# Level products of a blocked triangular inverse: from 64x64 weight tiles to 32x32 quarters with compact masks

## The reference, cut to what matters

```python
def step(s, inp):
    r_t, w_t, k_t, v_t, kk_t, a_t = inp
    sa = jnp.einsum('bhvk,bhk->bhv', s, -kk_t)
    s = s * w_t[:, :, None, :] + sa[..., None] * (kk_t * a_t)[:, :, None, :] + v_t[..., None] * k_t[:, :, None, :]
    return s, jnp.einsum('bhvk,bhk->bhv', s, r_t)
```

## Time and profile before

| quantity | value |
|---|---|
| median of 3 runs | 1657.73 us (1657.66 to 1657.81) |
| the profiled execution | 1657.09 us, span 1655.3 us |
| mean granted clock of TensorE | 0.948 |
| PE matmuls | 1465.5 us busy, 89% of the span, 17678 instructions |
| PE loads | 930.4 us, 56% |
| DVE | 605.6 us, 37%, 1520 instructions |
| ACT | 528.1 us, 32% |
| POOL | 264.7 us, 16% |
| level products of levels 1 to 4 (L2485), 881 to 1240 us | 3072 matmuls, 114.8 us busy |
| their mask on DVE (L2346) | 64 instructions, 0.52 to 0.56 us |

### The profile page before, as it was taken

The page is one execution under the profiler, slowest core; times in us unless marked ns, Lnnn a source line. Parts: engine busy times, 40 slices in busy tenths (PEclk is TensorE's granted clock), DMA queues, the critical chain, the costliest instruction groups (busy, mean ns, idle before and its releaser), DMA issues. The chain is left out here.

```text
span 1655.3 us, 41184 instructions
## 1 busy us (share of the span) xinstructions
PE 1465.5 (89%) x17678; PEld 930.4 (56%) x17678; DVE 605.6 (37%) x1520; ACT 528.1 (32%) x1202; POOL 264.7 (16%) x260
## 2 busy tenths in 40 slices
PE   3998878878999999959998888888879779999997
PEld 1554557446555555535556777777755555555554
DVE  2003673243111111551214666666751511111116
ACT  3013553232121121220134666666541311111122
POOL 0000031002000000010034455556500100000010
PEclk9999899888999999979999999999988889999999
DMA  9324556737799999803210000000004469999992
GB/s 390 128 102 164 221 210 244 300 115 315 278 369 379 374 377 373 332 26 102 103 50 3 6 6 6 6 6 6 6 4 170 154 267 364 374 370 380 375 387 90
DMA packets 54037, 328.34 MB, mean 198 GB/s; under 512 B 6646, under 2 KB 10038, under 8 KB 18712
## 3 DMA queue, kind: packets, MB, share of 16 engines
q1 hardware_dynamic: 43632, 290.07, 45.9%
q0 software_dynamic: 5184, 18.88, 2.9%
q10 hardware_dynamic: 5096, 17.58, 2.7%
HBM read 304.35 MB, written 22.16 MB: 197 GB/s over the span
## 5 line engine op out<-in xcount | busy, mean ns | idle before, releaser
L1398 PE MATMUL ps<-ring,arena 128*64 128x256 f32 x2048 | 244.3, 387 | 6.0 <-ACT arena L1513 4.9
L1398 PEld LDWEIGHTS ps<-ring,arena 128*64 128x64 f32 x2048 | 142.4, 138 | 97.2 <-issue 36.6
L298 PE MATMUL ps<-HT,ring 128*128 128x384 f32 x544 | 181.3, 497 | 14.2 <-PEq L367 8.2
L298 PEld LDWEIGHTS ps<-HT,ring 128*128 128x128 f32 x544 | 105.8, 195 | 89.5 <-issue 20.3
L1408 PE MATMUL ps<-ring,arena 128*32 128x128 f32 x4096 | 133.9, 278 | 0.0
L1602 DVE TENSOR_TENSOR arena<-arena,ps 64x256 f32<-64x256 f32 (+1 forms) x128 | 40.6, 357 | 254.0 <-ACT arena L1519 254.0
L1434 PE MATMUL ps<-ring,arena 128*64 128x512 f32 x512 | 129.9, 605 | 0.0
L1518 ACT ACTIVATE arena<-ps 64x256 f32<-64x256 f32 x64 | 24.1, 377 | 311.3 <-PE ps L1398 311.3
L1408 PEld LDWEIGHTS ps<-ring,arena 128*32 128x32 f32 x4096 | 107.8, 111 | 27.0 <-issue 25.4
L298 PE MATMUL ps<-arena,ring 128*128 128x384 f32 x256 | 85.4, 498 | 18.8 <-DVEq L2053 18.8
L1526 ACT ACTIVATE arena<-ps 32x256 f32<-32x256 f32 x128 | 47.8, 374 | 160.3 <-PE ps L1434 159.2
(11 more groups left out here) (358 smaller groups left out, 2244.2 us busy)
## 6 DMA issues: line engine op xcount, KB each, us to landing
ring<-wstream SPq DMA_DIRECT2D x272, 1024.0 KB, 7.5
moe_rows<-arena ACTq DMA_DIRECT2D x28, 384.0 KB, 7.1
arena<-moe_tokens POOLq DMA_DIRECT2D x12, 512.0 KB, 14.7
moe_rows<-arena ACTq DMA_DIRECT2D x4, 512.0 KB
consts<-cst ACTq DMA_DIRECT2D x1, 1655.0 KB, 17.1
XT<-xT ACTq DMA_DIRECT2D x1, 1536.0 KB, 11.1
yT<-HT SPq DMA_DIRECT2D x3, 384.0 KB, 3.2
arena<-wa SPq DMA_DIRECT2D x1, 1024.0 KB, 4.9
```

What stands on the lines that cost most here:

```text
L298: mm = pe.matmul(bank(m % 8), w[:, k, m % 2 * P:m % 2 * P + P], rhs[:, k, :], start=k == 0, stop=k == KC - 1)
L1398: mm = pe.matmul(bank(h, 256)[HD * x:HD * x + HD], TOKE[:, k, 0:MANY], w[:, kk, x, :], start=k == 0, stop=k == KC - 1)
```

## The change

The products of levels 1 to 4 are issued by `quarters_pe`: for each of the 6 chunks four matmuls, one for each quarter of 32 partitions, with the 32x32 diagonal block as weights and 32 columns, written to the same quarter of PSUM and of the array. The output is 32 columns a chunk, not 64. PF becomes half as wide (T words, in place of 2 T). The masks of levels 1 to 4, which stand in the constants as 64x64 patterns, are folded once into LM, 32 columns wide, by 8 additions on DVE ahead of the first pair. `left_dve` and `right_dve` then work on 192 elements a partition, contiguous in PSUM.

```diff
-        ATF, PF, ODF = (area(take(U2), U2) for _ in range(3))
+        ATF = area(take(U2), U2)
+        PF = area(take(T), T, d=2, n=NCH, j=32)
+        LM = area(take(8 * 32), 8 * 32, v=4, d=2, j=32)
+        take(T - 8 * 32)
+        ODF = area(take(U2), U2)
...
             def left_dve(dve, c, n, d):
                 dve.wait_ge(s_ll, c * NLL + (2 * n - 1 + d))
+                p_ = bank(LEFT_BANKS[d], NCH * 32).rearrange("p (n j) -> p n j", j=32)
                 if n == NLEV:
-                    p_ = bank(LEFT_BANKS[d], NCH * 32).rearrange("p (n j) -> p n j", j=32)
-                    dve.tensor_copy(dn(PF)[:, d, :, 0:32], p_).then_inc(s_ls, 1)
+                    dve.tensor_copy(PF[:, d], p_).then_inc(s_ls, 1)
                     return
-                mask = msk1(C_LEV + 2 * (n - 1) * CH, d)
-                dve.tensor_tensor(dn(PF)[:, d].rearrange("p n (b j) -> p n b j", b=2),
-                                  bank(LEFT_BANKS[d], NCH * HD).rearrange("p (n b j) -> p n b j", b=2, j=32),
-                                  mask.rearrange("p n (b j) -> p n b j", b=2), ALU.mult).then_inc(s_ls, 1)
+                dve.tensor_tensor(PF[:, d], p_, LM[:, n - 1, d].unsqueeze(1).broadcast_to([P, NCH, 32]),
+                                  ALU.mult).then_inc(s_ls, 1)
...
-                once = bank(RIGHT_BANKS[d], NCH * HD).rearrange("p (n b j) -> p n b j", b=2, j=32)[:, :, 0]
-                dve_o(dve.tensor_tensor(DTC[:, d], DTC[:, d], once, ALU.subtract))
+                dve_o(dve.tensor_tensor(dtc, dtc, bank(RIGHT_BANKS[d], NCH * 32), ALU.subtract))
...
                 dve_o.inc(dve.memset(DTF, 0.0))
+                dve.wait_ge(s_xm, 6)
+                for n in range(1, NLEV):
+                    for d in range(2):
+                        at = C_LEV + 2 * (n - 1) * CH + d * CH
+                        dve_o.inc(dve.tensor_tensor(LM[:, n - 1, d], C[:, at:at + 32], C[:, at + 32:at + CH], ALU.add))
...
-            def each(pe, o, left, right, d):
+            def quarters_pe(pe, o, left, right, d):
                 for n in range(NCH):
-                    for h in halves:
-                        mm = pe.matmul(bank(o, HD, HD * n)[h].rearrange("p (b j) -> p b j", b=2), dn(left)[h, d, n],
-                                   right[h, d, n].unsqueeze(1).broadcast_to([HD, 2, 32]), start=True, stop=True)
+                    for q in range(4):
+                        rows = slice(32 * q, 32 * q + 32)
+                        mm = pe.matmul(bank(o, 32, 32 * n)[rows], left(rows, n, q % 2), right[rows, d, n], start=True, stop=True)
                 return mm
...
-                    mm = each(pe, LEFT_BANKS[d], AF, DC, d)
+                    mm = quarters_pe(pe, LEFT_BANKS[d], lambda rows, m, i: dn(AF)[rows, d, m, 32 * i:32 * i + 32], DC, d)
...
-                    mm = each(pe, RIGHT_BANKS[d], PF, DTC, d)
+                    mm = quarters_pe(pe, RIGHT_BANKS[d], lambda rows, m, i: PF[rows, d, m], DTC, d)
```

More of the change, by code:

```diff
@@ L2509, in right_pe @@
                             k, i = HD * g + 32 * d, HD * g + 32 * (1 - d)
-                            mm = pe.matmul(bank(RIGHT_BANKS[d], 32, 32 * m)[k:k + 32], dn(PF)[i:i + 32, d, m, 0:32],
+                            mm = pe.matmul(bank(RIGHT_BANKS[d], 32, 32 * m)[k:k + 32], PF[i:i + 32, d, m],
                                            DTC[i:i + 32, d, m], start=True, stop=True)
```

## The result

The changed kernel takes 1686.8 us, the median of four runs (1685.66 to 1688.57), against 1657.77 for the kernel before: a ratio of 1.0174 [1.0156, 1.0191]. It is 29 us slower. The forecast was 1656.5 with a range of 1647 to 1664. The profiled execution took 1686.16 us.

A forecast was written before the change was run, and what follows sets the result against it. No engine bounds a pair alone; a chain of four legs does. 0.85 us times 8 pairs plus the first and last pair's extra gave 7.8 us, less 6.6 for the clock: 1.2 gained, 1656.5 us, range 1647 to 1664.

The forecast's parts named there:

- a call at 0.38 us: PE's level calls: 48 quarter matmuls, four side by side, take 0.38 us, 0.32 less a call, 16 calls a pair.
- leg B: Crossed matmuls between mask L2385 and the LoRA products: overlap with level calls lost, 3.8 us against 3.25, 0.55 lost.
- the clock: Emptier PE at the pair's end and around level 4 brings more clock falls, giving back 6.6 us together.
- rival 3: Quarters don't run four abreast, or the 60-column rule holds: calls stay at 0.70 us, 4 us slower, 1662; chance 0.08.
- Leg A and D: Pair's start up to mask L2385: 0.35 us gained; level 4 at its end: 0.85 us gained a pair.
- Leg C: ACT's work from the sigmoids to L2193, which level 4's first left call awaits: 5.6 us, follows as before.
- rival 2: Thin quarter calls make clock falls last on, one of double length per pair more, 8.4 us: 1665; chance 0.20.
- Rival 1's second case: Clock falls no more often than today and crossed matmuls keep their overlap: 1641; rival 1's chance 0.30.

The follow-up runs named there:

- e3: Changed kernel with 64 columns (the 32 read twice) in each quarter product, DVE reading the first 32: 1676.31 us, ratio 1.0109.
- e5: Changed kernel plus 16 unused products of 128x128 by 32 columns at the head of the stage on PE: 1686.78 us (one run).
- e9: Kernel before plus three times 320 unused products at the stage's head (64x64 by 64, 32x32 by 32, 32x32 by 64): 1713.75 us (one run).
- e4: Kernel before with DVE's left step masking only the first 32 columns of each block, PE unchanged, outputs not the reference's: 1651.28 us, ratio 0.9957.
- e10: Kernel before with all four calls of level 2 as quarters by 64 columns, DVE unchanged: 1664.37 us, ratio 1.0039.
- after: The changed kernel itself, measured against the kernel before: 1686.8 us, ratio 1.0174.
- e8: Kernel before with quarters by 32 columns and the compact mask in level 4 alone: 1661.32 us, ratio 1.0022.
- e1: Kernel before with its 24 level products of 64x64 weights a call by 32 columns, the mask reading them twice: 1715.32 us, ratio 1.0345.
- e6: Changed kernel plus unused 128x128 by 256 products after level 3 and in the last two scan steps, and a wait for ACT: 1695.49 us, ratio 1.0230.
- e2: Kernel before with each level product cut into two matmuls of 64x64 weights by 32 columns, 48 a call: 1778.71 us, ratio 1.0721.

## Why the prediction was wrong

**The step that failed.** The sum took a call at 0.38 us, "if the call waits for nothing else", and had no term for what feeds it. PE's supply of instructions was that something. It is the largest item: 18.8 us of breaks in the changed kernel (e3, e5, e9 and the packets' landings show what they are). Two terms that the sum did have were too small as well, leg B and the clock (below). Alone, where the stream has room before it, a call is as forecast: in pair 3 one follows the other in the call's own pace,

```profile
1045.13 0.49 PEld L2492 LDWEIGHTS ps<-ring,arena 32*32 32x32 f32 x47 [0.55 <-issue]
...
1045.54 0.51 PEld L2492 LDWEIGHTS ps<-ring 32*32 32x32 f32 x45
```

0.41 us apart. Four quarters do run side by side, and rival 3 is out. But 16 level calls of a pair, with 24 loads and 24 matmuls more each, bring 768 instructions into it, three more blocks of 256, and in the dense stretches, where calls already ran at the supply's pace, it has no reserve for them.

**The sum in seven pairs.** The first three terms are each read from a run or a row that has it:

| term | us | from |
|---|---|---|
| DVE's shorter left step | -4.8 | e4 |
| crossed leg, 7 x (4.01 - 3.25) | +5.3 | timeline of pair 3; e10 |
| breaks | +18.8 | trace of after; e3, e5, e9 |
| remainder: lower clock, less what shorter calls give | +11.1 | difference to 30.4 |

The table takes every us of break as a us of time, and its last term is not measured alone. It fits after less e3: 14.2 us, of which the shorter crossed leg takes 3.6 off and the larger breaks put 4.0 on, leaving 13.8. e3 against e4, the same clock but for 0.01, closes nearly by itself: 21.0 us in seven pairs, against 8.9 (leg) plus 14.8 (breaks, of the whole stage). e5 shows how far the split can be trusted: with 17.4 us of breaks in other places its seven pairs are 21.0 us over before, which would leave 3.1 for the remainder, not 11.1. That breaks are a large part holds in both; the shares belong to one placement.

**Leg A and D, DVE.** The left step is 0.349 us, forecast 0.35. Of the forecast 7.8 us, DVE alone gives 6.6. PE's shorter calls add nothing that any run shows: e8, the place of the 0.85 a pair, is no faster.

**Leg B.** Right in kind: nothing overlaps, and each change of shape leaves a gap ([0.17 <-issue]). Its size was 4.01, not 3.8, since the loads of a call are 0.51 and the gap 0.17 and not 0.12. The loss is 0.76 a pair instead of 0.55.

**Leg C** is untouched: ACT's L2193 starts its work after the LoRA products as before, 5.06 us behind its first sigmoid (1045.23 to L2197 at 1050.29; 1029.30 to 1034.36 in the earlier trace rows).

**The clock.** Twelve falls that cost about 1 us each were forecast, 6.6 us more than today. They came, and last longer. Read in steps of 0.25 us, the granted clock of the kernel before falls to its lower level five times between 881 and 1220 us, for 3.2 to 6.8 us each; in the changed kernel fifteen times, for 3.2 to 17.2 us. In pair 3 it falls at 1034.5 for 3.5 us and at 1051.5, around level 4, for 7.0: the place was forecast rightly, and other pairs have 13.5 to 17 us there. Over the 409 us, 106 us more stand at 1.2 GHz. At the price of the earlier trace rows, 1.05 us for a leg of 5.55, that is some 20 us (an estimate), less what shorter calls return. This was rival 2, with the chance 0.20, but at the price of one longer fall a pair (1665). e1 shows how much the columns alone can do; whether the breaks, in which PE stands still, lengthen the falls is not parted here: e3 has 17 of them at a clock of 0.96. (Rival 1's second case adds up to 1640, not 1641; nothing hangs on it.)

**The page's rule.** The Trainium skill, "TensorEngine Tiling (Array Packing)", Instruction Overhead, says that a matmul with fewer than 60 columns takes as long as one with 60. It was weighed and rightly not followed for quarters: the loads of 48 are busy for 0.51 us by 32 columns and 0.71 by 64 (after and e10), and a call takes 0.41 us against 0.69 before. With 64x64 weights the run agrees with it: halving the columns bought nothing (e1).

## What to carry to other kernels

Before cutting matmuls into smaller ones, count the instructions: compare 256 of PE's, loads and matmuls together, with the time they now take, and if that is near 3.6 us, a finer cut buys breaks and not time. Ask also which neighbours of another line share the tile shape, because their overlap ends when the shape changes. And read the granted clock after columns are taken away: here even useless ones were worth keeping (e1: 0.95 to 0.77). An edit on PE and one on DVE that come together should be priced apart: here the DVE part was worth 6.6 us, and no complete version run here could keep it.

## What the runs showed of the hardware

- Instructions reach PE in blocks of 256, one each 3.5 to 3.75 us in a dense stretch (e9), and a stream of small matmuls that needs them faster stops between blocks for 0.2 to 2.4 us (after, e5, e6, e9). The place of the stop follows the count of instructions ahead (e5: 32 matmuls more, 32 places earlier), and PE goes on 1.2 to 1.6 us behind the landing of a packet of the instruction queue (all breaks of six runs).
- 64x64 weights by 32 columns are no faster than by 64: 0.73 us against 0.69 for 24 (e1), and a second matmul with the same weights has a load of its own, so that 48 take 1.62 us (e2, clock 0.92).
- With equal counts and equal call times, half the columns in the level calls took the granted clock of the stage from 0.95 to 0.77 (e1), and quarters by 64 columns stand at 0.96 where quarters by 32 stand at 0.82 (e3).
- Off-diagonal and diagonal 64x64 tiles overlap across calls and lines. With another shape between them the same work takes 4.01 to 4.52 us and not 3.25, at 0.17 us a change.
